# Reordering the hand-written queues at the entry of the first MLP product: token splits, weight splits and one split moved to GpSimd

## The chip, the cores and the metric

The kernel runs on one core of a Trainium2 chip. The metric is the device time of one execution, in microseconds (us). Before the change it was 1467.71 us, the median of three runs (1466.81 to 1469.4).

## The reference

One encoder layer over two sequences (1024 and 512 tokens, model width 1024) with shared weights, and a final RMSNorm. The part around the change is the end of the mixer and the start of the MLP:

```
x = x + gate1 * (mix @ w_out)
h = rms_norm(x, g_mlp) * (1 + scale2) + shift2
ff = square(relu(h @ w_ff1)) @ w_ff2          # w_ff1: 1024 x 4096
x = x + gate2 * ff
```

Everything is float32.

## The kernel before, in words

**Arithmetic.** Float32 products are made from three fp32r products: each operand v is split into v_hi (a copy in fp32r) and v_lo = v - v_hi, and each tile costs the matmuls w_lo*v_hi, w_hi*v_lo, w_hi*v_hi (`three_more`, L968 to L970). Both MLP products use a Strassen-Winograd scheme on 2x2 blocks with seven products, P1, P5, P6, P2, P7, P3, P4 in the order in which TensorE does them. The operands of the seven products are blocks of h or differences of such blocks.

**Chunks.** The 1536 tokens are three chunks of 512, done in the order 0, 2, 1. In the output projection TensorE makes eight groups of matmuls for a chunk (d = 0 to 7). For each group VectorE adds the result to x (L1949), ScalarE squares it (L1113, `square`), VectorE adds the squares up (L1611, `add_square`). The sum of squares of a chunk is summed over partitions by TensorE (`norm_sum`), becomes 1/rms by a ScalarE root and a VectorE reciprocal (L1617), and is spread over the partitions by TensorE (`norm_spread`). Then VectorE (`norm_apply`, L1910) and ScalarE (`modulate`, L1399) make h of the chunk, eight tiles of 128x512.

**Token operands, in two parts.** Part 0 is made from chunks 0 and 2 (operands of 128x2048), and is complete while TensorE still works on chunk 1. Part 1 is made from chunk 1 (128x1024). For each part: four differences on VectorE (`token_sum`, L1920 to L1929), seven hi copies on ScalarE (`token_hi`, L1409), seven lo subtractions on VectorE (`token_lo`, L1937). The hi copies share one counter, so `HI_ORDER` must repeat the order in which ScalarE makes them.

**Weights.** For each job q, SyncE loads four blocks of w_ff1; GpSimd makes four differences (`w1_add`, L2260 to L2274), ScalarE the hi copies (`split_w1_hi`, L1425), GpSimd the lo subtractions (`w1_split_lo`, L2284), all 128x512.

**Jobs.** Job 0 uses part 0 alone (512 columns); jobs 1 to 4 and most later ones use both parts (768 columns). TensorE makes P1 to P4 of a job; ScalarE copies the results of P1, P6, P7, P4 out of PSUM (`ff1_out`, L1434, counter `ff1_copy`); VectorE combines all of it in eleven steps, U2, C11, B11, C22, B22, C12, B12, T1, T3, T2, T4 (`hid_out`, L1985 to L2015, counter `hid_step`). P1, P6, P7 and P4 of a job take the same PSUM banks one after the other. These waits tie the engines together at the border between job 0 and job 1:

```
elif i == P2: after(pe, ff1_copy, 4 * q)
...
else: pe.wait_ge(ff1_copy, 4 * q + {P6: 1, P7: 2, P4: 3}[i])     # in ff1_product
...
after(act, hid_step, NHID * (q - 1) + step)                      # in ff1_out
ff1_out(q, P1, S_B11, T1)
```

So P6 of job 1 waits for the copy of P1 of job 1, and that copy, which writes over the slot `S_B11`, waits for step T1 of job 0. The copy of P6 waits for T2 of job 0, and TensorE's P1, P5 and P3 of job 1 wait for C11, C22 and C12 of job 0. All products of job 1 wait for the last `norm_apply` of chunk 1.

The order of the work on each engine is written out by hand. VectorE, ScalarE and GpSimd each take their instructions strictly in that order. For the change the relevant pieces are: the loop over the groups of chunk 1 (`for d in range(KD)` with i == 2 on VectorE; `square(n, k)` with n == NN + 2 on ScalarE), and the straight code behind it. `square(n, k)` with k > 2 waits until `add_square` has taken the buffer of k - 2, and `add_square(n, k)` waits for `square(n, k)`. The difference for P6 on GpSimd (L2268) waits in job 0 for group 4 of chunk 1 (`out_mm` at 2 * KD + 5).

Of the kernel before, what the change touches and what calls it, by code (L numbers as in the profile page):

```python
# [44 lines left out]
KD = D // P  # L45
# [24 lines left out]
P1, P5, P6, P2, P7, P3, P4 = range(7)  # L70
U2, C11, B11, C22, B22, C12, B12, T1, T3, T2, T4 = range(1, 12)

HI_ORDER = ((P1, P2, P3, P5, P6, P7, P4), (P1, P5, P6, P2, P3, P7, P4))
S_B11, S_T2, S_T3, S_T4, S_B21, S_T1, S_B22 = range(7)
NHID = 11
NSTEP = 7 * NPAIR // GF
# [37 lines left out]
def build_encoder(nc, vec_d, xT_d, w_mod_d, w_mod1_d, w_in_d, w_gate_d, w_four_d, w_out_d, w_ff1_d, w_ff2_d,  # L114
# [608 lines left out]
    def _(pe):  # L723
# [282 lines left out]
        for q in range(NJ):  # L1006
            for i in range(7):
                ff1_product(q, i)
                if q == 0 and i == P5:
                    norm_sum(2 * NN - 1)  # L1010
                elif q == 0 and i == P6:
                    norm_spread(2 * NN - 1)

        def fin_sum(h):
# [78 lines left out]
    def _(act):  # L1093
# [346 lines left out]
        for n in range(NN, 2 * NN):  # L1440
            if n > NN:
                root(n - 1)
            square(n, 0)
            if n > NN:
                modulate(n - 1)
            for k in range(1, KD):
                if n == NN + 1 and k == 3:
                    token_hi(P1, 0)
                    token_hi(P2, 0)
                elif n == NN + 2 and k == 2:  # L1450
                    token_hi(P3, 0)
                    split_w1_hi(0, P1)
                    token_hi(P5, 0)
                elif n == NN + 2 and k == 3:
                    token_hi(P6, 0)
                elif n == NN + 2 and k == 4:
                    token_hi(P7, 0)
                    split_w1_hi(0, P5)
                elif n == NN + 2 and k == 5:
                    split_w1_hi(0, P6)  # L1460
                    split_w1_hi(0, P2)
                elif n == NN + 2 and k == 6:
                    token_hi(P4, 0)
                square(n, k)

        def split_w2_hi(n):

# [55 lines left out]
        split_w1_hi(0, P3)  # L1523
        ff1_out(0, P6, S_T3, T2)
        split_w1_hi(0, P4)
        modulate(2 * NN - 1, range(4))
        split_w1_hi(1, P1)
        modulate(2 * NN - 1, range(4, KD))
        ff1_out(0, P7, S_B22, T2)
        token_hi(P1, 1)  # L1530
        split_w1_hi(1, P5)
        token_hi(P5, 1)
        split_w1_hi(1, P6)
        token_hi(P6, 1)
        split_w1_hi(1, P2)
        token_hi(P2, 1)
        ff1_out(0, P4, S_B21, T4)
        token_hi(P3, 1)
        for q in range(1, NJ):
            ff1_out(q, P1, S_B11, T1)  # L1540
            if q == 1:
                token_hi(P7, 1)
                token_hi(P4, 1)
            split_w1_hi(q, P7)
            split_w1_hi(q, P3)
            ff1_out(q, P6, S_T3, T2)
            split_w1_hi(q, P4)
            if q + 1 < NJ:
                split_w1_hi(q + 1, P1)
            else:  # L1550
                split_w2_hi(0)
                split_hin_hi(0)
            ff1_out(q, P7, S_B22, T2)
            if q + 1 < NJ:
                split_w1_hi(q + 1, P5)
                split_w1_hi(q + 1, P6)
            ff1_out(q, P4, S_B21, T4)
            if q + 1 < NJ:
                split_w1_hi(q + 1, P2)
# [30 lines left out]
    def _(dve):  # L1590
# [348 lines left out]
        for i in range(NCH):  # L1939
# [3 lines left out]
            for d in range(KD):  # L1943
# [12 lines left out]
                    add_square(NN + i, d - 1)  # L1956
                if i == 2 and d == 1:
                    token_sum(1, 0)
                    token_sum(2, 0)
                elif i == 2 and d == 2:  # L1960
                    token_lo(P1, 0)
                elif i == 2 and d == 3:
                    token_sum(3, 0)
                elif i == 2 and d == 4:
                    token_lo(P5, 0)
                elif i == 2 and d == 5:
                    token_sum(4, 0)
                elif i == 2 and d == 6:
                    token_lo(P6, 0)
            add_square(NN + i, KD - 1)  # L1970

        def hid_out(q, step):
# [128 lines left out]
            dve.wait_ge(norm_bc, 2 * NN + 2)  # L2101
            final(tiles, HTOK + CH, T, bank[7][:, 0:QC])

        token_lo(P2, 0)
        token_lo(P7, 0)
        rstd(2 * NN - 1)
        token_lo(P3, 0)
        norm_apply(2 * NN - 1, range(4))
        token_lo(P4, 0)
        norm_apply(2 * NN - 1, range(4, KD))  # L2110
        hid_out(0, U2)
        hid_out(0, C11)
        token_sum(1, 1)
        token_sum(2, 1)
# [2 lines left out]
        hid_out(0, C22)  # L2117
        token_lo(P5, 1)
        token_sum(3, 1)
        token_sum(4, 1)  # L2120
        for step in (B22, C12, B12, T1):
            hid_out(0, step)
        token_lo(P6, 1)
        token_lo(P2, 1)
        hid_out(0, T3)
        hid_out(0, T2)
        token_lo(P7, 1)
        token_lo(P3, 1)
        token_lo(P4, 1)
        hid_out(0, T4)  # L2130
        for q in range(1, NJ):
            for step in (U2, C11, B11):
                hid_out(q, step)
# [57 lines left out]
    def _(pool):  # L2191
# [51 lines left out]
        for i in range(16):  # L2243
# [2 lines left out]
                               wo_hi[WO_ORDER[i]][:].rearrange("p k m -> p (k m)"), ALU.subtract  # L2246
                               ).then_inc(wo_lo_done, 1)

        def w1_add(q, i):

            o = 7 * q + i
# [44 lines left out]
        for q in range(NJ):  # L2296
            w1_split_lo(q, P1)
            w1_add(q, P5)
            w1_add(q, P6)
            w1_split_lo(q, P5)  # L2300
            w1_split_lo(q, P6)
            w1_split_lo(q, P2)
            w1_add(q, P7)
            w1_add(q, P3)
            w1_split_lo(q, P7)
            w1_split_lo(q, P3)
            w1_split_lo(q, P4)
# [69 lines left out]
```

## Time and profile before

| | |
|---|---|
| median of three runs | 1467.71 us |
| range | 1466.81 to 1469.4 us |
| the profiled execution's own time | 1466.81 us |
| its span, from the first to the last instruction | 1465.0 us |
| mean granted TensorE clock | 0.990 |
| TensorE busy with matmuls | 1410.0 us (96%) |
| VectorE / ScalarE / GpSimd busy | 816.4 / 591.7 / 506.8 us |

TensorE is called PE in the rows, its weight loads PEld, VectorE DVE, ScalarE ACT, GpSimd POOL, and SyncE's queue SPq. A row of the timeline is: start, duration, engine, line, operation, output and inputs, and in brackets the idle time of the engine before it and what ended it. Wait tables infer the releaser from semaphore events; where an instruction waits for several things, they name the one that came last by the profile. Durations of two instructions in a row on one engine overlap by about 0.1 us, so the start-to-start distance is what a queue costs.

### The profile page before, as it was taken

To read this page: it belongs to the slowest core of one execution; us is meant where nothing else is said; L and a number is where in the kernel's file an instruction comes from. 1 tells how busy PE (TensorE), PEld (TensorE's weight loads), DVE (VectorE), ACT (ScalarE), POOL (GpSimd) and SP (SyncE) were. 2 spreads that over 40 slices of the span, in tenths; PEclk is the share of its full clock that TensorE was granted. 3 is DMA by queue.
4 is the path that set the end of the run, shared out by engine and by line. 5 is a ranking of instruction groups with operands and counts; after the bars stand their busy time and mean duration, and the time that the engine had idled before them with its cause. 6 is when DMAs were issued, how large, how long until landed. Compare 5 with 4: busy or idle time off the path is not lost.

```text
span 1465.0 us, 18563 instructions
## 1 busy us (share of the span) xinstructions
PE 1410.0 (96%) x7576; PEld 1190.6 (81%) x7576; DVE 816.4 (56%) x765; ACT 591.7 (40%) x704; POOL 506.8 (35%) x292
## 2 busy tenths in 40 slices
PE   3899999999999989999999999999999999999996
PEld 1576777788888878888888888888888888888885
DVE  5755687685536896353445344542655443344575
ACT  6448887846344443233222222242232222423231
POOL 6211111017200555565554555442223222232221
PEclk9899999999999999999999999999999999999998
DMA  9243431012512223433333333379998433445532
GB/s 370 87 159 133 156 121 36 15 58 84 203 58 87 87 88 138 153 133 130 119 115 147 142 119 117 147 244 390 393 377 312 159 144 144 161 180 207 209 134 86
DMA packets 75411, 232.35 MB, mean 159 GB/s; under 512 B 5696, under 2 KB 9920, under 8 KB 66368
## 3 DMA queue, kind: packets, MB, share of 16 engines
q1 hardware_dynamic: 75328, 231.17, 42.6%
q8 instruction: 61, 1.00, 0.3%
q14 instruction: 22, 0.18, 0.0%
HBM read 166.14 MB, written 65.01 MB: 158 GB/s over the span
## 4 chain that ended last, share of the span: by engine, by line
PE 52%; DVE 5%; issue 3%; SPq 2%; ACT 1%; DMA 1%; POOL 0%; DVEq 0%; ACTq 0%; POOLq 0%
PE bank L968 17%; PE bank L969 17%; PE bank L970 17%; DMA w_raw<-in_w_ff 1%; SPq L687 1%; DVE hin_lo L2036 1%; ACT hin_hi L1490 1%; DVE x L2086 1%; SPq L627 1%; DVE x L2052 0%; DVE hid L2000 0%; DVE w_raw L2031 0%; DVE w_raw L2029 0%; DVE w_raw L2027 0%; POOL w_lo L2284 0%
## 5 line engine op out<-in xcount | busy, mean ns | idle before, releaser
L968 PE MATMUL bank<-hin_hi,w_lo 128*128 128x512 f32 (+1 forms) x896 | 302.4, 337 | 1.8 <-DVE hin_lo L2036 1.8
L969 PE MATMUL bank<-hin_lo,w_hi 128*128 128x512 f32 (+1 forms) x896 | 301.7, 337 | 0.0
L970 PE MATMUL bank<-hin_hi,w_hi 128*128 128x512 f32 (+1 forms) x896 | 301.1, 336 | 0.0
L2036 DVE TENSOR_TENSOR hin_lo<-hin,hin_hi 128x3072 fp32r<-128x3072 f32 x28 | 140.9, 5031 | 208.1 <-ACT hin_hi L1490 208.1
L2292 POOL TENSOR_TENSOR w_lo<-w_raw,w_hi 128x2048 fp32r<-128x2048 f32 x28 | 129.5, 4625 | 330.5 <-ACT w_hi L1478 329.0
L968 PEld LDWEIGHTS bank<-hin_hi,w_lo 128*128 128x128 f32 x896 | 170.1, 190 | 21.0 <-issue 2.8
L969 PEld LDWEIGHTS bank<-hin_lo,w_hi 128*128 128x128 f32 x896 | 170.1, 190 | 17.8 <-issue 0.2
L970 PEld LDWEIGHTS bank<-hin_hi,w_hi 128*128 128x128 f32 x896 | 169.9, 190 | 17.9
L1478 ACT ACTIVATE w_hi<-w_raw 128x2048 fp32r<-128x2048 f32 x28 | 53.6, 1916 | 288.8 <-PE bank L970 181.6
L2284 POOL TENSOR_TENSOR w_lo<-w_raw,w_hi 128x512 fp32r<-128x512 f32 x51 | 73.9, 1449 | 206.6 <-ACT w_hi L1425 206.6
L1434 ACT ACTIVATE hid<-bank 128x768 f32<-128x768 f32 (+2 forms) x68 | 52.5, 772 | 170.4 <-PE bank L970 163.3
L968 PE MATMUL bank<-t_hi,w_lo 128*128 128x512 f32 (+1 forms) x320 | 112.2, 351 | 6.3 <-DVE t_lo L1937 3.7
L969 PE MATMUL bank<-t_lo,w_hi 128*128 128x512 f32 (+1 forms) x320 | 112.1, 350 | 0.0
L970 PE MATMUL bank<-t_hi,w_hi 128*128 128x512 f32 (+1 forms) x320 | 111.6, 349 | 0.0
L2284 POOL TENSOR_TENSOR w_lo<-w_s,w_hi 128x512 fp32r<-128x512 f32 x68 | 103.2, 1530 | 10.0 <-ACT w_hi L1425 6.5
L1985 DVE TENSOR_TENSOR hid<-bank,hid 128x768 f32<-128x768 f32 (+2 forms) x17 | 15.5, 910 | 147.1 <-ACT hid L1434 147.1
L2207 POOL TENSOR_TENSOR win_lo<-win_raw,win_hi 128x1024 fp32r<-128x1024 f32 x12 | 30.8, 2565 | 192.0 <-ACT win_hi L1136 192.0
L968 PE MATMUL bank<-hi_f,w_lo 128*128 128x512 f32 (+1 forms) x256 | 86.6, 338 | 1.9 <-POOL w_lo L2284 1.9
L968 PE MATMUL bank<-hi_r,w_lo 128*128 128x512 f32 (+1 forms) x256 | 87.2, 341 | 0.0
L1425 ACT ACTIVATE w_hi<-w_s 128x512 fp32r<-128x512 f32 x68 | 42.9, 632 | 109.3 <-POOL w_s L2274 47.6
L969 PE MATMUL bank<-lo_r,w_hi 128*128 128x512 f32 (+1 forms) x256 | 86.9, 339 | 0.0
L969 PE MATMUL bank<-lo_f,w_hi 128*128 128x512 f32 (+1 forms) x256 | 86.5, 338 | 0.0
(271 smaller groups left out, 3204.2 us busy)
## 6 DMA issues: line engine op xcount, KB each, us to landing
hin<-hid_all SPq DMA_DIRECT2D x28, 1536.0 KB, 6.6
hid_all<-hid SPq DMA_DIRECT2D x105, 384.0 KB, 2.5
w_raw<-in_w_ff SPq DMA_DIRECT2D x36, 1024.0 KB, 9.0
w_raw<-in_w_ff SPq DMA_DIRECT2D x68, 256.0 KB, 2.8
mod_raw<-in_w_mod SPq DMA_DIRECT2D x16, 1024.0 KB, 5.1
x<-in_xT SPq DMA_DIRECT2D x5, 2048.0 KB, 14.0
w_sums<-w_raw SPq DMA_DIRECT2D x8, 1024.0 KB, 15.4
w_raw<-w_sums SPq DMA_DIRECT2D x8, 1024.0 KB, 10.4
```

The lines of the kernel that those rows point to most:

```text
L627: sp.dma_start(w2_raw[m % RAWS][:], src).then_inc(ld_w2[m % RAWS], 16)
L968: pe.matmul(out, w_lo, v_hi, start=first, stop=False, skip_group_check=True)
L969: pe.matmul(out, w_hi, v_lo, start=False, stop=False, skip_group_check=True)
L970: return pe.matmul(out, w_hi, v_hi, start=False, stop=last, skip_group_check=True)
L1425: act.activation(w1_hi[o % 4][:], src[:], ACT.Copy).then_inc(w1_hi_done, 1)
L1434: act.activation(hid[j][:, c0:c1], ps[:, buf + c0:buf + c1], ACT.Relu if i == P4 else ACT.Copy).then_inc(ff1_copy, 1)
L1478: act.activation(w2_hi[n % 2][:], w2_raw[m % RAWS][:], ACT.Copy).then_inc(w2_hi_done, 1)
L1985: m = dve.tensor_tensor(slot[S_T3][:, cols], out_of(1), slot[S_T3][:, cols], ALU.add)
L2036: dve.tensor_tensor(hin_lo[n % 3][:].rearrange("p t n -> p (t n)"), hin[n % 3][:].rearrange("p t n -> p (t n)"), hin_hi[n % 3][:].rearrang ...
L2207: pool.tensor_tensor(win_lo[win_of(j)][:].rearrange("p k m -> p (k m)"), raw[:], win_hi[win_of(j)][:].rearrange("p k m -> p (k m)"), ALU.s ...
L2284: pool.tensor_tensor(w1_lo[o % 4][:], src[:], w1_hi[o % 4][:], ALU.subtract).then_inc(w1_lo_done, 1)
L2292: pool.tensor_tensor(w2_lo[n % 2][:].rearrange("p t n -> p (t n)"), w2_raw[m % RAWS][:].rearrange("p t n -> p (t n)"), w2_hi[n % 2][:].rea ...
```

## The change

Work is moved between places in the queues of ScalarE, VectorE and TensorE, and one subtraction moves to another engine. No work is added or removed.

- ScalarE, part 0: the hi copies come in the order P1, P2, P5, P3, P6, P7, P4. In front of the square of tile 3 of chunk 1 there are now the weight hi copies of P1, P5, P6 and P2 of job 0 and the token hi copies of P3 and P6; P7's is in front of the square of tile 4, and P4's behind the last square.
- VectorE, part 0: the lo subtraction of P2 moves into the loop, the differences move to later groups, the lo subtraction of P7 leaves VectorE; GpSimd does it, between its weight subtraction for P2 and its difference for P7 of job 0.
- TensorE: the spreading of the last norm comes behind P2 of job 0 instead of P6.
- VectorE, part 1: `norm_apply` is done in one piece, behind U2 of job 0; the five lo subtractions of P6, P2, P7, P3 and P4 come in front of T1 of job 0, and T1, T3, T2, T4 close the sequence. C12 and B12 stand between the subtractions of P2 and P7.
- ScalarE, part 1: the copy of P7 of job 0 comes after four tiles of `modulate` instead of eight; weight hi copies come in front of the token hi copies; the token hi copies of P7 and P4 come in front of the copy of P1 of job 1.

```diff
-HI_ORDER = ((P1, P2, P3, P5, P6, P7, P4), (P1, P5, P6, P2, P3, P7, P4))
+HI_ORDER = ((P1, P2, P5, P3, P6, P7, P4), (P1, P5, P6, P2, P7, P3, P4))
...
                 if q == 0 and i == P5:
                     norm_sum(2 * NN - 1)
-                elif q == 0 and i == P6:
+                elif q == 0 and i == P2:
                     norm_spread(2 * NN - 1)
...
                 elif n == NN + 2 and k == 2:
-                    token_hi(P3, 0)
-                    split_w1_hi(0, P1)
                     token_hi(P5, 0)
                 elif n == NN + 2 and k == 3:
+                    split_w1_hi(0, P1)
+                    token_hi(P3, 0)
+                    split_w1_hi(0, P5)
+                    split_w1_hi(0, P6)
+                    split_w1_hi(0, P2)
                     token_hi(P6, 0)
                 elif n == NN + 2 and k == 4:
                     token_hi(P7, 0)
-                    split_w1_hi(0, P5)
-                elif n == NN + 2 and k == 5:
-                    split_w1_hi(0, P6)
-                    split_w1_hi(0, P2)
-                elif n == NN + 2 and k == 6:
-                    token_hi(P4, 0)
                 square(n, k)
+        token_hi(P4, 0)
...
         split_w1_hi(0, P4)
-        modulate(2 * NN - 1, range(4))
+        modulate(2 * NN - 1, range(2))
         split_w1_hi(1, P1)
+        modulate(2 * NN - 1, range(2, 4))
+        ff1_out(0, P7, S_B22, T2)
         modulate(2 * NN - 1, range(4, KD))
-        ff1_out(0, P7, S_B22, T2)
+        split_w1_hi(1, P5)
         token_hi(P1, 1)
-        split_w1_hi(1, P5)
+        split_w1_hi(1, P6)
         token_hi(P5, 1)
-        split_w1_hi(1, P6)
+        ff1_out(0, P4, S_B21, T4)
+        split_w1_hi(1, P2)
         token_hi(P6, 1)
-        split_w1_hi(1, P2)
         token_hi(P2, 1)
-        ff1_out(0, P4, S_B21, T4)
+        token_hi(P7, 1)
         token_hi(P3, 1)
+        token_hi(P4, 1)
         for q in range(1, NJ):
             ff1_out(q, P1, S_B11, T1)
-            if q == 1:
-                token_hi(P7, 1)
-                token_hi(P4, 1)
...
                 if i == 2 and d == 1:
                     token_sum(1, 0)
+                elif i == 2 and d == 2:
                     token_sum(2, 0)
-                elif i == 2 and d == 2:
                     token_lo(P1, 0)
                 elif i == 2 and d == 3:
                     token_sum(3, 0)
-                elif i == 2 and d == 4:
                     token_lo(P5, 0)
                 elif i == 2 and d == 5:
                     token_sum(4, 0)
+                    token_lo(P6, 0)
                 elif i == 2 and d == 6:
-                    token_lo(P6, 0)
+                    token_lo(P2, 0)
...
-        token_lo(P2, 0)
-        token_lo(P7, 0)
+        token_lo(P3, 0)
         rstd(2 * NN - 1)
-        token_lo(P3, 0)
-        norm_apply(2 * NN - 1, range(4))
         token_lo(P4, 0)
-        norm_apply(2 * NN - 1, range(4, KD))
         hid_out(0, U2)
+        norm_apply(2 * NN - 1)
         hid_out(0, C11)
...
         token_lo(P5, 1)
         token_sum(3, 1)
+        hid_out(0, B22)
         token_sum(4, 1)
-        for step in (B22, C12, B12, T1):
-            hid_out(0, step)
         token_lo(P6, 1)
         token_lo(P2, 1)
-        hid_out(0, T3)
-        hid_out(0, T2)
+        for step in (C12, B12):
+            hid_out(0, step)
         token_lo(P7, 1)
         token_lo(P3, 1)
         token_lo(P4, 1)
-        hid_out(0, T4)
+        for step in (T1, T3, T2, T4):
+            hid_out(0, step)
...
+        def token_lo(i, part):                                   # on GpSimd
+
+            v, v_hi, v_lo = token_operand(i, part)
+            pool.wait_ge(op_hi, hi_count(i, part))
+            pool.wait_ge(op_sum, 4 * part + {P1: 1, P7: 3, P3: 3, P4: 4}[i])
+            pool.tensor_tensor(v_lo, v, v_hi, ALU.subtract).then_inc(op_lo[i], 1)
...
             w1_split_lo(q, P2)
+            if q == 0:
+                token_lo(P7, 0)
             w1_add(q, P7)
```

## Rows read from the trace of the kernel before

**Rows 1.** The page: busy time, share of the span, instructions.

```profile
PE 1410.0 (96%) x7576; PEld 1190.6 (81%) x7576; DVE 816.4 (56%) x765; ACT 591.7 (40%) x704; POOL 506.8 (35%) x292
```

**Rows 2.** Waits of TensorE, whole span: total us, times, longest us.

```profile
PE bank L968 <- DVE t_lo L1937: 3.7, 1, 3.7
PE bank L968 <- issue: 2.6, 1, 2.6
PE bank L968 <- POOL w_lo L2284: 1.9, 1, 1.9
```

**Rows 3.** Windows: engines' busy time, then granted clock, DMA share, GB/s.

```profile
515.00:520.00 5.00, 3.37 (x10) 2.73 (x11) 4.90 (x6) 5.00 (x8) 3.16 (x3) 0.77 0.00 0
650.00:655.00 5.00, 5.00 (x30) 5.00 (x31) 3.26 (x7) 1.09 (x3) 3.70 (x3) 0.66 0.43 135
```

**Rows 4.** Timeline of TensorE around job 0 and job 1.

```profile
500.75 0.95 PE L739 MATMUL bank<-ones,n_acc 128*128 128x1 f32 x8
...
516.63 0.47 PE L968 MATMUL bank<-t_hi,w_lo 128*128 128x512 f32 x1 [2.64 <-issue]
516.94 0.40 PE L969 MATMUL bank<-t_lo,w_hi 128*128 128x512 f32 x1
517.18 0.39 PE L970 MATMUL bank<-t_hi,w_hi 128*128 128x512 f32 x1
...
518.83 0.63 PE L969 MATMUL bank<-t_lo,w_hi 128*128 128x512 f32 x1
519.26 0.63 PE L970 MATMUL bank<-t_hi,w_hi 128*128 128x512 f32 x1
...
533.25 0.47 PE L968 MATMUL bank<-t_hi,w_lo 128*128 128x512 f32 x1 [3.68 <-DVE t_lo L1937]
```

**Rows 5.** Timeline of VectorE from the last norm to step T1 and behind it.

```profile
506.44 0.74 DVE L1910 SCALAR_TENSOR_TENSOR n_t<-x,amp,bank 128x512 f32<-128x512 f32 x1
...
515.10 0.68 DVE L1985 TENSOR_TENSOR hid<-bank,hid 128x512 f32<-128x512 f32 x1
...
530.35 1.64 DVE L2004 TENSOR_TENSOR hid<-hid,hid 128x512 f32<-128x512 f32 x1
531.91 1.21 DVE L1937 TENSOR_TENSOR t_lo<-t_s,t_hi 128x1024 fp32r<-128x1024 f32 x1
533.05 1.21 DVE L1937 TENSOR_TENSOR lo_r<-h_r,hi_r 128x1024 fp32r<-128x1024 f32 x1
```

**Rows 6.** Timeline of ScalarE.

```profile
468.30 0.63 ACT L1425 ACTIVATE w_hi<-w_raw 128x512 fp32r<-128x512 f32 x1 [1.72 <-PE bank L728]
468.84 1.90 ACT L1409 ACTIVATE t_hi<-t_s 128x2048 fp32r<-128x2048 f32 x1
470.64 0.61 ACT L1113 ACTIVATE tmp<-x 128x512 f32<-128x512 f32 x1
...
532.07 0.81 ACT L1434 ACTIVATE hid<-bank 128x768 f32<-128x768 f32 x1 [7.19 <-DVE hid L2004]
```

**Rows 7.** Timeline of GpSimd in the loop over chunk 1.

```profile
479.32 1.30 POOL L2268 TENSOR_TENSOR w_s<-w_s,w_raw 128x512 f32<-128x512 f32 x1 [7.30 <-PE bank L728]
```

**Rows 8.** Timeline of VectorE in the loop over chunk 1.

```profile
474.10 0.74 DVE L1949 SCALAR_TENSOR_TENSOR x<-bank,mod,x 128x512 f32<-128x512 f32 x1
474.76 0.68 DVE L1611 TENSOR_TENSOR n_acc<-n_acc,tmp 128x512 f32<-128x512 f32 x1
475.36 2.28 DVE L1926 TENSOR_TENSOR h_f<-h_r,h_f 128x2048 f32<-128x2048 f32 x1
...
497.02 0.69 DVE L1611 TENSOR_TENSOR n_acc<-n_acc,tmp 128x512 f32<-128x512 f32 x1 [0.17 <-ACT tmp L1113]
```

**Rows 9.** Timeline of GpSimd and VectorE in the second product, near 1000 us.

```profile
987.94 3.36 DVE L2036 TENSOR_TENSOR hin_lo<-hin,hin_hi 128x3072 fp32r<-128x3072 f32 x1 [6.21 <-ACT hin_hi L1490]
...
996.65 4.62 POOL L2292 TENSOR_TENSOR w_lo<-w_raw,w_hi 128x2048 fp32r<-128x2048 f32 x1 [10.44 <-ACT w_hi L1478]
...
999.26 5.24 DVE L2036 TENSOR_TENSOR hin_lo<-hin,hin_hi 128x3072 fp32r<-128x3072 f32 x1 [7.96 <-ACT hin_hi L1490]
```

## The prediction

> **What bounds the kernel now.** I read the page first: TensorE is busy 96% of the span [rows 1], so an order of instructions can only win or lose where TensorE idles. The wait table of TensorE gives two waits in the stretch of the change, 2.6 and 3.7 us, and one of 1.9 us in a later job [rows 2]. The timeline places them: 2.64 us before P4 of job 0, which starts at 516.63, and 3.68 us before P6 of job 1, which starts at 533.25 [rows 4]. Behind the first one the granted clock falls: 0.77 of full speed from 515 to 520, and matmuls start 0.43 us apart instead of 0.24 [rows 3, 4], the lower level, 1.2 GHz, instead of 2.4. About 8 matmuls are hit, some 1.6 us. The 1.9 us wait is followed by such a stretch too (0.66 from 650 to 655) [rows 3].
>
> Then the question is which wait ends last. The table names a split, t_lo at L1937, for 533.25. The code and ScalarE's timeline say otherwise: P6 of job 1 needs `ff1_copy` 5, the copy of P1 of job 1. That copy stood on ScalarE for 7.19 us and began at 532.07, released by L2004, step T1 of job 0 [rows 6]; T1 ran from 530.35 to 531.99 [rows 5], the copy ended at 532.88. The split of P6 for part 1 ended at 533.12, but the first matmuls of P6 are on part 0 and don't need it. So the path that sets the end runs along VectorE up to T1, through ScalarE's copy, into TensorE at 533.25. Everything that TensorE gains or loses before it ends in that wait: the 2.64 us and the slow stretch of P4 are already hidden by it. Behind it TensorE has no wait until the one of 1.9 us, which moves along with TensorE, since that job's weights wait on TensorE's own progress.
>
> **The change part by part.** The measure is the time at which T1 of job 0 is done.
>
> *T1 behind the splits of part 1.* VectorE's stream from U2 at 515.10 to the end of T1 at 531.99 took 16.9 us [rows 5]. U2 moves in front of the norm (-0.6). Five 1024-wide subtractions (P6, P2, P7, P3, P4) come in front of T1. One costs 1.14 us of queue (531.91 to 533.05), so 5 x 1.14 = 5.7; where GpSimd is in the way one can take double, which is the upper bound, 11.4. I take 5.7, because GpSimd's next work (the weight subtractions of P7 of job 1) hangs behind the copy that hangs behind T1, so it is idle then. Net: +5.1.
>
> *P7's split on GpSimd.* It takes 4.62 us there by the row of the same shape [rows 9], against 2.28 for a 2048-wide operation on VectorE [rows 8]. VectorE is spared 2.2 us. But while GpSimd works, a VectorE operation with two inputs in SBUF stands still: the 3072-wide subtraction takes 3.36 us alone and 5.24 us when it began at 999.26 beside GpSimd's 4.62 from 996.65, and it ended at 1004.50, 3.23 after GpSimd's end at 1001.27. It waited for all of the rest of it [rows 9]. The Trainium skill (SBUF — State Buffer, "Who interferes with whom") has this as a rule: the port pair that VectorE and GpSimd share is an exclusive lock for a whole instruction, and a VectorE instruction with two SBUF inputs needs it. The trace agrees (1.9 us of waiting). By that rule 4.62 us can be lost to the add behind it; if the two only shared bandwidth, about half of that.
>
> *The new order on ScalarE.* The weight hi copy of P6 now stands in front of the square of tile 3. It needs the difference that GpSimd may begin at 479.32 at the earliest, when group 4 is done, and that takes 1.30 [rows 7]. Worked through, with 0.66 for an add to x, 0.60 for an add of squares, 2.2 for a 2048-wide operation on VectorE [rows 8], 0.54 and 1.80 for the short and the long hi copies on ScalarE [rows 6]:
> - Group 2 is done at 468.30 [rows 6]. VectorE does x, add, difference 2, split P1, x, add, difference 3: 0.66 + 0.6 + 2.2 + 2.2 + 0.66 + 0.6 + 2.2 = 9.1, and about 1.7 for two GpSimd operations in the way: 479.1. Then the split of P5 to 481.4. GpSimd's difference waits for it and is done at 482.6.
> - ScalarE: two weight copies, the hi of P6 (1.8), square 3 to about 486.1, the hi of P7 to 487.9, square 4 to 488.5. VectorE has stood idle for the add of square 3 from 482 to 486.1.
> - GpSimd takes P7's split at 488.0 and holds the port to 492.6. The add of square 4 (ready at 488.6) waits for it: 493.2. Difference 4, split P6, x of group 6, add (behind a GpSimd operation, 1.8), split P2, x of group 7: 502.8. The last two adds: 504.8. Before, the last add ended at 497.71 [rows 8].
> - TensorE would have begun the norm's sum at 500.75 [rows 4]; it begins at 504.8, a new wait of 3.8 us, hidden like the 2.64. P6 (behind ScalarE's late copy of P1, 506.0) and P2 at 2.7 each and the spreading end at 512.1. `norm_apply` begins then instead of at 506.44 [rows 5]; its eight tiles, with the copies between them on ScalarE, take about 6.5, to 518.6. Before, its end with P4's split in the middle was 515.10. Net: +3.5. If nothing early is late, the sum is at 500.75, the spreading at 507.7, the tiles end at 514.2, and this term is -0.9; if the clock falls in the wait before the sum, it is +5.1.
>
> *TensorE's slow stretch.* P6 of job 1 will start about 533.25 + 5.1 + 3.5 = 541.9. P5 ends near 532, so the idle time is nearly 10 us, more than either wait of before. I expect the lower clock level behind it, now on the path: +1.6 (8 matmuls at 0.19 more each, the measured stretch [rows 4]). The bounds are 0, as behind the 3.68 us wait, and 1.7.
>
> *Costed at nothing.* The earlier copy of P7 takes the 2.64 us wait away, but P4 of job 0 is hidden by the wait before P6. The weight hi copies of job 1 moved forward, and the loads of job 2, which SyncE sends behind T4 of job 0: T4 ends at about the same time as before, and TensorE needs them over 8 us later. The copy of P6 of job 1 waits for T2 and a store, and both are due before the late P6 ends. The cover of all of this is the wait before P6; without it they would cost up to 2 us each.
>
> The sum against the profiled execution's own time: 1466.81 + 5.1 + 3.5 + 1.6 = **1477.0 us**. The median of the runs is 0.9 above that execution, which the range takes in.
>
> **Rivals.**
> - *The early part stays hidden.* If GpSimd's difference gets in front of P5's split (it is late by only 0.2 us in my working) or P7's split finds the port free, the early term lies between -0.9 and +1.5: 1466.8 + 5.1 + 0.3 + 1.6 gives about 1473.8, down to 1471.0. For it: the race is close, and adds on VectorE are short. Against: the square of tile 3 still can't come before 484 or so.
> - *No change.* From U2 to T1 VectorE's work alone is six 1.14 us units, eight short steps of 0.6 and 0.5 between dependent ones, 12.1 us, against the 16.9 that it took: 4.8 us went to GpSimd's turns at the port. If the new order met none of them, norm_apply would end at 514.2 and T1, with C11, eleven 1.14 us units of differences and splits and six short steps, at 514.2 + 0.6 + 12.5 + 3.6 + 0.8 = 531.7, against 531.99. That is 1466.5. It needs every port wait gone, with GpSimd's work unchanged.
> - *Faster.* The wait table is right and the code's reading wrong: the split L1937 releases P6 of job 1, not T1. Then the split, with P7's 2.2 us off VectorE, is done at about 530.9 instead of 533.1, and 2.2 us are gained: 1464.6. It decides if P6 of job 1 starts before T1 has ended. Against it stands a counter that TensorE must wait for.
>
> **How the numbers follow.** My working: 0.65. Early part hidden: 0.20. No change: 0.09. Faster: 0.04, and 0.02 for a still later chain. About 0.2% (2.9 us) is what a measurement of this kernel can tell from no change. Faster 0.04, same 0.10, slower 0.86. The likeliest case spans 1475 (no slow stretch) to 1480.4 (two slow stretches and the median's 0.9 on top). The range goes down to 1471.0 for the second case and leaves about 0.15 out.
>
> **What would show it.** Right: one long wait of TensorE, 8 to 11 us, before P6 of job 1 at 540 to 543, released by the copy at L1434; T1 (L2004) directly behind L1937 rows, ending near 540.6; a wait of 3 to 4 us before the sum at L739 near 504; a GpSimd row of 128x2048 with 4.6 us near 488 and an add (L1611) of over 4 us beside it; no wait before P4 of job 0. Wrong: P6 of job 1 before 536, the sum at 501, or the slow stretch missing behind the long wait.

## The result, and the profile after

The changed kernel took 1481.59 us (median of six runs, 1479.63 to 1485.63) against 1468.57 us for the kernel before on the same chip: ratio 1.0094, 95% interval 1.0076 to 1.0112. It is slower, as forecast, but by more than forecast: 1477.0 had been named, with 1480.4 as the upper end. The profiled execution is not one of these six: it took 1484.28 us, its span 1482.5, 17.5 longer than the 1465.0 of before.

Waits of TensorE in the changed kernel, whole span (engine, line, releaser: us in total, times, longest us). They answer to [rows 2]:

```profile
PE bank L968 <- ACT hid L1434: 10.2, 1, 10.2
...
PE bank L739 <- DVE n_acc L1609: 3.2, 1, 3.2
...
PE bank L968 <- DVE lo_f L1935: 2.2, 1, 2.2
PE bank L968 <- POOL w_lo L2286: 1.9, 1, 1.9
```

Timeline of TensorE in the changed kernel, the counterpart of [rows 4]:

```profile
509.32 1.87 PE L739 MATMUL bank<-ones,n_acc 128*128 128x1 f32 x8 [3.25 <-DVE n_acc L1609]
511.05 0.77 PE L968 MATMUL bank<-t_hi,w_lo 128*128 128x512 f32 x1
...
514.61 0.63 PE L970 MATMUL bank<-t_hi,w_hi 128*128 128x512 f32 x1
515.04 0.53 PE L968 MATMUL bank<-t_hi,w_lo 128*128 128x512 f32 x1
...
549.76 0.77 PE L968 MATMUL bank<-t_hi,w_lo 128*128 128x512 f32 x1 [10.16 <-ACT hid L1434]
550.33 0.63 PE L969 MATMUL bank<-t_lo,w_hi 128*128 128x512 f32 x1
```

The norm's sum (L739) has a wait of 3.25 us in front of it, and takes 1.87 us instead of the 0.95 of [rows 4]. P6 of job 1 starts at 549.76 behind 10.16 us of waiting, and the table now names ScalarE's copy at L1434, the releaser that the code had given for the kernel before too.

VectorE, the counterpart of [rows 5, 8]:

```profile
461.25 0.75 DVE L1947 SCALAR_TENSOR_TENSOR x<-bank,mod,x 128x512 f32<-128x512 f32 x1 [2.32 <-PE bank L728]
...
490.77 0.83 DVE L1609 TENSOR_TENSOR n_acc<-n_acc,tmp 128x512 f32<-128x512 f32 x1 [4.16 <-ACT tmp L1113]
491.52 0.74 DVE L1947 SCALAR_TENSOR_TENSOR x<-bank,mod,x 128x512 f32<-128x512 f32 x1
493.10 4.61 DVE L1609 TENSOR_TENSOR n_acc<-n_acc,tmp 128x512 f32<-128x512 f32 x1 [0.84 <-ACT tmp L1113]
...
519.63 0.75 DVE L1908 SCALAR_TENSOR_TENSOR n_t<-x,amp,bank 128x512 f32<-128x512 f32 x1 [2.26 <-PE bank L746]
...
526.00 0.68 DVE L1987 TENSOR_TENSOR hid<-bank,hid 128x512 f32<-128x512 f32 x1
...
546.69 1.22 DVE L1935 TENSOR_TENSOR t4b_lo<-t4b_s,t4b_hi 128x1024 fp32r<-128x1024 f32 x1
547.82 0.68 DVE L2002 TENSOR_TENSOR hid<-hid,hid 128x512 f32<-128x512 f32 x1
```

ScalarE and GpSimd of the same kernel:

```profile
487.19 0.63 ACT L1425 ACTIVATE w_hi<-w_s 128x512 fp32r<-128x512 f32 x1 [5.47 <-POOL w_s L2270]
...
490.05 0.62 ACT L1113 ACTIVATE tmp<-x 128x512 f32<-128x512 f32 x1
...
548.59 0.81 ACT L1434 ACTIVATE hid<-bank 128x768 f32<-128x768 f32 x1 [7.68 <-issue]
```

```profile
484.01 3.08 POOL L2270 TENSOR_TENSOR w_s<-w_s,w_raw 128x512 f32<-128x512 f32 x1 [3.02 <-PE bank L728]
...
492.55 4.60 POOL L2249 TENSOR_TENSOR lo_f<-h_f,hi_f 128x2048 fp32r<-128x2048 f32 x1 [1.50 <-ACT hi_f L1409]
```

Read together, these show the foreseen chain. GpSimd's difference begins where it did before (484.01, less the 4.70 us of which the next paragraph tells, is 479.31; before it was 479.32 [rows 7]), but it takes 3.08 us instead of 1.30, beside VectorE's split of P5, which ran until 485.95, so it ends late. ScalarE's weight copy waits 5.47 us for it. VectorE's add of square 3 waits 4.16 us, and the add of square 4 stands 4.61 us beside GpSimd's 4.60 us split. At the end, T1 (L2002) stands directly behind the splits, and the copy at L1434 behind T1.

**What the trace adds.** The first add to x of chunk 1 starts at 461.25, but the kernel before had it earlier:

```profile
456.55 0.75 DVE L1949 SCALAR_TENSOR_TENSOR x<-bank,mod,x 128x512 f32<-128x512 f32 x1 [2.32 <-PE bank L728]
```

Nothing ahead of this point was changed. The windows say where the 4.70 us went (columns as in [rows 3]); first the kernel before, then the changed one:

```profile
320.00:325.00 5.00, 5.00 (x40) 4.85 (x41) 5.00 (x9) 5.00 (x9) 0.00 (x0) 1.00 0.01 3
325.00:330.00 5.00, 5.00 (x25) 4.05 (x23) 5.00 (x8) 3.21 (x7) 2.75 (x3) 1.00 0.00 0
```

```profile
320.00:325.00 5.00, 5.00 (x28) 5.00 (x28) 5.00 (x9) 5.00 (x9) 0.00 (x0) 0.57 0.01 3
325.00:330.00 5.00, 5.00 (x18) 4.32 (x18) 5.00 (x8) 3.23 (x7) 1.67 (x2) 0.50 0.00 0
...
510.00:515.00 5.00, 5.00 (x15) 4.17 (x16) 4.70 (x3) 3.05 (x8) 2.93 (x2) 0.50 0.93 304
```

From 320 to 330 the granted clock is at its lower level in the changed kernel's profile, in untouched code. So I measure by a **distance**: from the first add to x of chunk 1 on VectorE to the start of P6 of job 1 on TensorE. It was 533.25 - 456.55 = 76.70 us and is 549.76 - 461.25 = 88.51 us. The 17.5 us are 4.70 ahead of it, 11.81 in it, and 1.0 behind it. The distance ends where P6 starts, so it doesn't hold what the clock costs behind that start. Where that matters I give a second measure, from the same first add to the end of the span: 1008.45 us before, 1021.25 changed, 12.8 more.

### The profile page after: what moved, and what is told of

Same layout as the page of the kernel before. It is cut to its first block, busy times and chain, and to the rows that moved or that the text cites. A ratio compares the mean times of both kernels' runs of the same rounds, so it can differ in the third digit from the quotient of the medians.

```text
span 1482.5 us, 18562 instructions
## 1 busy us (share of the span) xinstructions
PE 1417.1 (96%) x7576; PEld 1197.4 (81%) x7576; DVE 809.4 (55%) x764; ACT 591.4 (40%) x704; POOL 503.4 (34%) x293
## 4 chain that ended last, share of the span: by engine, by line
PE 58%; DVE 2%; issue 2%; ACT 1%; POOL 0%; DVEq 0%; ACTq 0%; POOLq 0%
PE bank L968 19%; PE bank L969 19%; PE bank L970 19%; DVE x L2084 1%; ACT hin_hi L1488 1%; DVE w_raw L2029 0%; DVE hin_lo L2034 0%; POOL w_lo L2286 0%; DVE fin_acc L2068 0%; DVE x L2050 0%; DVE fin_acc L2060 0%; ACT fin_sq L1502 0%; PE bank L1025 0%; ACT fin_b L1510 0%; POOL w_s L2272 0%
## 5 line engine op out<-in xcount | busy, mean ns | idle before, releaser
L1434 ACT ACTIVATE hid<-bank 128x768 f32<-128x768 f32 (+2 forms) x68 | 52.5, 772 | 181.2 <-PE bank L970 173.6
L968 PE MATMUL bank<-t_hi,w_lo 128*128 128x512 f32 (+1 forms) x320 | 113.4, 354 | 11.2 <-ACT hid L1434 10.2
L2286 POOL TENSOR_TENSOR w_lo<-w_s,w_hi 128x512 fp32r<-128x512 f32 x68 | 97.4, 1444 | 18.6 <-ACT w_hi L1425 15.1
L1998 DVE SCALAR_TENSOR_TENSOR hid<-hid 128x768 f32<-128x768 f32 (+2 forms) x51 | 86.5, 1696 | 1.7
## 6 DMA issues: line engine op xcount, KB each, us to landing
w_raw<-w_sums SPq DMA_DIRECT2D x8, 1024.0 KB, 10.2
```

Source lines behind the costliest of these rows:

```text
L968: pe.matmul(out, w_lo, v_hi, start=first, stop=False, skip_group_check=True)
L1434: act.activation(hid[j][:, c0:c1], ps[:, buf + c0:buf + c1], ACT.Relu if i == P4 else ACT.Copy).then_inc(ff1_copy, 1)
L1998: m = dve.scalar_tensor_tensor(t, t, 0.0, t, ALU.max, ALU.mult)
L2286: pool.tensor_tensor(w1_lo[o % 4][:], src[:], w1_hi[o % 4][:], ALU.subtract).then_inc(w1_lo_done, 1)
```

## The experiments

Line numbers differ by a few between kernels. The kernel before had a median of 1469.58 us (13 runs) beside the first four kernels, 1469.89 (23 runs) beside the two with fillers and the two at the end, and 1469.71 (23 runs) beside the other three.

**The late part alone.** The kernel before, with VectorE's order behind `token_sum(3, 1)` and the token hi copies of part 1 in the changed kernel's order:

```diff
+        hid_out(0, B22)
         token_sum(4, 1)
-        for step in (B22, C12, B12, T1):
-            hid_out(0, step)
         token_lo(P6, 1)
         token_lo(P2, 1)
-        hid_out(0, T3)
-        hid_out(0, T2)
+        for step in (C12, B12):
+            hid_out(0, step)
         token_lo(P7, 1)
         token_lo(P3, 1)
         token_lo(P4, 1)
-        hid_out(0, T4)
+        for step in (T1, T3, T2, T4):
+            hid_out(0, step)
```

> The kernel before with the late part alone: on VectorE the five lo subtractions of part 1 stand in front of T1 of job 0, with ScalarE's token hi copies of P7 and P4 in front of the copy of P1 of job 1. Mark for all runs: D, from the start of VectorE's add to x of group 0 of chunk 1 to the start of P6 of job 1 on TensorE; 76.7 us in the kernel before, 88.5 in the changed one. Theory (T1 is what P6 of job 1 waits for, and it is moved behind 5 x 1.14 us): D 81.8 to 82.5, the wait before P6 of job 1 grows from 3.7 to about 9 us, the norm's sum on TensorE without a new wait, and with a slow stretch behind the wait the time is 7 us above before. Rival (the early part carries the loss, the splits in front of T1 are free because VectorE has slack): D 76.7 and no change of time.

Measured: 1475.39 us, ratio 1.005 (1.0033 to 1.0067); distance 82.38, +5.7. T1 behind the splits costs what five splits were priced at, 5.7, with nothing early in play. TensorE:

```profile
539.19 0.77 PE L968 MATMUL bank<-t_hi,w_lo 128*128 128x512 f32 x1 [10.76 <-ACT hid L1434]
```

**T1 put back in the changed kernel** (the diff above, reversed, on the VectorE side).

> The changed kernel with VectorE's late sequence put back (B22, C12, B12, T1 in front of the five lo subtractions), all else as changed. Theory: T1 ends about 6 us earlier, D 82 to 83, wait before P6 of job 1 about 4 us, the wait of 3 us before the norm's sum still there with its slow stretch; time about 6 us above before and 7 below the changed kernel. Rival (early part carries the loss): D stays near 88.

Measured: 1477.22 us, ratio 1.0054 (1.0035 to 1.0073); distance 82.20, 6.3 less than in the changed kernel. To the end of the span it is 4.5 less (1016.76): the slow stretch behind P6's start is longer here. The early part stays: the sum waits 3.25 us, as in the changed kernel.

**P7's split back on VectorE in the changed kernel.**

```diff
+        token_lo(P7, 0)
         token_lo(P3, 0)
         rstd(2 * NN - 1)
...
-            if q == 0:
-                token_lo(P7, 0)
             w1_add(q, P7)
```

> The changed kernel with the lo subtraction of P7 of part 0 back on VectorE, behind the last add of squares. Theory (GpSimd's 4.6 us hold the port against the add of square 4, and that delays the sum): the add of square 4 takes 0.7 instead of 4.6, the norm's sum starts with a wait under 1 us and no slow stretch behind it; VectorE pays 2.2 us for the subtraction; D 83 to 86, time 7 to 10 us above before. Rival (only ScalarE's new order delays the sum): the wait before the sum stays near 3 us, D 88 or more.

Measured: 1476.05 us, ratio 1.0055 (1.0034 to 1.0076); distance 83.09, 5.4 less, and, with a longer slow stretch behind P6's start here too, 3.8 less to the end of the span (1017.48). VectorE:

```profile
485.85 0.82 DVE L1609 TENSOR_TENSOR n_acc<-n_acc,tmp 128x512 f32<-128x512 f32 x1 [4.17 <-ACT tmp L1113]
486.60 0.74 DVE L1947 SCALAR_TENSOR_TENSOR x<-bank,mod,x 128x512 f32<-128x512 f32 x1
488.18 0.69 DVE L1609 TENSOR_TENSOR n_acc<-n_acc,tmp 128x512 f32<-128x512 f32 x1 [0.84 <-ACT tmp L1113]
```

The wait for square 3 is there (4.17), the next add is short (0.69 instead of 4.61), and TensorE's sum has no wait and takes 0.95 us. So the idle time that ScalarE's order causes doesn't by itself delay the sum.

**The weight copies back behind squares 4 and 5 on ScalarE in the changed kernel.**

```diff
                     token_hi(P3, 0)
-                    split_w1_hi(0, P5)
-                    split_w1_hi(0, P6)
-                    split_w1_hi(0, P2)
                     token_hi(P6, 0)
                 elif n == NN + 2 and k == 4:
                     token_hi(P7, 0)
+                    split_w1_hi(0, P5)
+                elif n == NN + 2 and k == 5:
+                    split_w1_hi(0, P6)
+                    split_w1_hi(0, P2)
```

> The changed kernel with the weight hi copies of P5, P6 and P2 of job 0 back at their places on ScalarE (in front of the squares of tiles 4 and 5). Theory (two causes in a row): VectorE's idle time of 4.2 us for the add of square 3 is gone, but GpSimd's subtraction of P7 still stands in front of an add or a difference; the sum is 1 to 2 us earlier than in the changed kernel, D 86 to 87.5. Rival (ScalarE's order is the whole early cause): the wait before the sum is gone and D is 83 or less. Rival (GpSimd is the whole cause): D unchanged, 88.5.

Measured: a median of 1481.86 us, ratio 1.0089 (1.0069 to 1.0108), hardly below the changed kernel's. The profiled execution took 1474.93 us, with a distance of 83.97, 4.5 less, more than expected. GpSimd's hold now falls on a split of VectorE, the sum waits 1.96 us instead of 3.25 and takes 1.05, not 1.87:

```profile
489.45 6.51 DVE L1936 TENSOR_TENSOR t_lo<-t_s,t_hi 128x2048 fp32r<-128x2048 f32 x1
```

```profile
502.93 1.05 PE L739 MATMUL bank<-ones,n_acc 128*128 128x1 f32 x8 [1.96 <-DVE n_acc L1610]
```

The other runs don't bear this out. The profiled one is the fastest of six; the others lie from 1479.70 to 1485.48. Whether the stretch behind the 1.96 us wait runs slow in the others is open, so what the weight copies' place is worth is not shown.

**Matmuls in the waits.** Two kernels keep TensorE busy in its waits with matmuls whose results nothing uses: `fill` sends `count` of them into a PSUM bank that is free at that time. The first kernel puts 14 before the norm's sum, the second also 38 before P6 of job 1.

```diff
+        def fill(count, i, q):
...
+            for n in range(count):
+                pe.matmul(bank[NBK][:], w1_hi[o % 4][:, 0:P], v_hi[:, n % FT], start=True, stop=True)
...
+                if q == 1 and i == P6:                 # the second kernel alone
+                    fill(38, P6, 1)
...
                 if q == 0 and i == P5:
+                    fill(14, P6, 0)
                     norm_sum(2 * NN - 1)
```

> The changed kernel with 14 extra matmuls of 512 columns on TensorE behind P5 of job 0, in the 3.25 us for which it waits for the last norm's sum (into the norm's own bank, which the sum writes anew). They add no work to VectorE, ScalarE or GpSimd. Theory (the wait is followed by the lower clock, and P6 and the sum at that clock delay the spreading, norm_apply and so T1): clock 1.00 from 510 to 515, sum in 0.95 us instead of 1.87, norm_apply 2 to 2.8 us earlier, D 85.7 to 86.5, time 2 to 3 us below the changed kernel. Rival (the lower clock there is hidden as it was at P4 in the kernel before): D 88.5.

> As the run before, and 38 more matmuls of 512 columns in the wait of 10 us before P6 of job 1. Theory: D as in the run before (85.7 to 86.5), no lower clock behind the wait, and the rest of the program from P6 of job 1 to the end takes 1.3 to 1.7 us less: time 3.5 to 4.5 us below the changed kernel. Rival (the clock behind that wait costs nothing, since a later wait takes it up): the rest takes as long as in the changed kernel.

Measured: 1478.63 us, ratio 1.0065 (1.0049 to 1.008), and 1477.81 us, 1.0056 (1.0039 to 1.0073). With the first filler the sum starts at the same distance (48.1) but takes 1.05 us, the first `norm_apply` tile comes at 56.06 instead of 58.38 behind the first add to x, and the whole distance is 86.20: 2.3 us less. More than half of this is lost again behind it. All 12 matmuls of 512 columns that open P6 of job 1, and four of 256 behind them, run at the lower clock here, where in the changed kernel it is the first six or seven; whether the filler has to do with that is open. To the end of the span 1020.25 us are left of 1021.25, a gain of 1.0, and the intervals of the two ratios overlap. So the trace shows what the sum's slow stretch costs on the path; the runs don't show a faster kernel. Windows of the first filler kernel, where the changed kernel has 0.50 behind its sum:

```profile
505.00:510.00 5.00, 4.71 (x24) 3.93 (x24) 5.00 (x4) 4.20 (x11) 2.95 (x2) 1.00 0.90 295
510.00:515.00 5.00, 5.00 (x22) 3.80 (x21) 2.98 (x5) 1.80 (x3) 2.31 (x2) 1.00 0.53 182
```

The second filler takes the slow stretch behind the long wait away as well. From the start of P6 of job 1 to the 1.93 us wait of the next job it is 116.60 us in the kernel before, 118.06 in the changed one, and 116.63 here. The distance stays at 86.25. To the end of the span it is 1017.62, 3.6 less than in the changed kernel, the lower end of what was expected.

**Both causes undone at once.** The changed kernel with the edits of the second and third experiments; ScalarE's and TensorE's new orders stay.

> The changed kernel with both causes undone: T1 of job 0 stands where it stood before the change, and VectorE makes the lo subtraction of P7 of part 0. ScalarE's and TensorE's new orders stay. Theory (two causes that add up, no third): from the first add to x of chunk 1 to the start of P6 of job 1, 88.5 us less 5.4 (P7 alone undone) less 6.3 (T1 alone undone) is 76.8 us, against 76.7 before the change; the sum starts on time at 44.2; the median is within 0.2% of the kernel before, ratio 0.999 to 1.002. Rival (the new ScalarE order costs something by itself, since putting it back gave 4.5 us): 78 to 80 us, the first norm_apply tile 2 to 3 us later than before, ratio 1.002 to 1.004.

Measured: 1470.08 us, ratio 1.0011 (0.9998 to 1.0024); distance 76.77. In the distance the two undo steps add up, and nothing is left: 88.51 - 6.3 - 5.4 = 76.8. To the end of the span it is 1009.63, 1.2 above the kernel before: behind its 3.88 us wait P6 meets the lower clock, where before it met none.

**P7's split on GpSimd in the kernel before**, all else as it was.

> The kernel before with one edit: the lo subtraction of P7 of part 0 goes from VectorE to GpSimd, between its weight subtraction for P2 and its difference for P7. Theory (the move costs nothing by itself; what costs is that in the changed kernel the split meets the adds of squares late and with the sum waiting on them): one add of squares takes over 4 us here too, but the sum starts on time at 44.2 us after the first add to x, norm_apply is not later than before (49.9) and may be 1 us earlier, and P6 of job 1 starts 75.7 to 76.7 us after it; ratio 0.998 to 1.001. Rival (the port hold always costs its 4.6 us less the 2.3 saved): P6 of job 1 at 78.5 to 79.5 us, the sum 2 to 4 us late, ratio 1.0015 to 1.003.

Measured: 1468.82 us, ratio 0.999 (0.9976 to 1.0003); distance 75.59, a little below what was expected, with the sum on time at 44.2. To the end of the span it is 1009.67, again 1.2 above the kernel before, for the same reason (P6 of job 1, below). An add is held here too, and it does no harm:

```profile
490.51 3.76 DVE L1611 TENSOR_TENSOR n_acc<-n_acc,tmp 128x512 f32<-128x512 f32 x1
```

**The changed kernel once more.**

> The changed kernel once more, unchanged. Theory (of its 17.5 us, 4.7 belong to a half-clock stretch at 321 to 331 us in code that the change does not touch, and it is drawn anew in each execution): in this profile the first add to x of chunk 1 starts at 456.3 to 456.8 us, or at 459.5 to 461.5 if the stretch is drawn again; in both cases P6 of job 1 starts 88 to 89 us behind it; the runs fall in two groups some 3 to 5 us apart, the fast one at 1479 to 1481. Rival (the stretch belongs to the changed kernel): the first add at 461.2 again and no run under 1482 beside it; or P6 of job 1 at another distance.

Measured: 1480.13 us, ratio 1.0081 (1.0061 to 1.01); the profiled execution took 1485.23. The slow stretch began earlier this time, the first add to x came at 462.14, P6 of job 1 at 550.53, distance 88.39. Windows of this execution:

```profile
315.00:320.00 5.00, 4.88 (x34) 4.88 (x35) 4.76 (x9) 4.08 (x7) 0.00 (x0) 0.78 0.00 0
320.00:325.00 5.00, 5.00 (x26) 5.00 (x25) 4.04 (x8) 4.31 (x7) 0.00 (x0) 0.50 0.02 3
```

My bounds for the start (459.5 to 461.5) were missed by 0.6. The rival, that no run would be under 1482, fell: the changed kernel has fourteen executions on record, twelve in the two medians and two more of 1484.28 (the first profiled one) and 1484.59. Seven lie from 1479.63 to 1480.74, one at 1482.43, six from 1484.28 to 1485.63. Both profiles happen to be of the slower kind, and without the stretch they would have taken 1484.28 - 4.70 = 1479.6 and 1485.23 - 5.6 = 1479.6 us.

**A version that is better than both.** The kernel before with P7's split on GpSimd, and with two differences of part 1 behind T1 instead of in front:

```diff
-        token_sum(3, 1)
-        token_sum(4, 1)
         for step in (B22, C12, B12, T1):
             hid_out(0, step)
+        token_sum(3, 1)
+        token_sum(4, 1)
```

> The kernel before with two edits: on VectorE, differences 3 and 4 of part 1 go behind T1 of job 0 (B22, C12, B12, T1, then the differences), and the lo subtraction of P7 of part 0 goes to GpSimd. Theory (T1 is the end of the path): T1 comes earlier by 2 x 1.14 us and some of GpSimd's turns, D 73.5 to 74.5, time 2 to 3 us below before. GpSimd's 4.6 us fall between 487 and 492, where one difference or add of squares waits, but the sum is not late. Rival (what is moved comes back as a wait for the split of P6, as the wait table names it): D 76 or more.

Measured: 1465.68 us, ratio 0.9975 (0.9963 to 0.9988), twelve runs. The distance is 72.40, less than expected, and 1005.06 to the end of the span (3.4 less than before), with a wait of 0.76 us in P6, where the split of its part 1 operand is now last:

```profile
528.84 0.47 PE L968 MATMUL bank<-t_hi,w_lo 128*128 128x512 f32 x1 [1.89 <-ACT hid L1434]
532.58 0.36 PE L968 MATMUL bank<-t_hi,w_lo 128*128 128x256 f32 x1 [0.76 <-DVE t_lo L1937]
```

A further kernel rewrote the order of VectorE from the last norm on, and ScalarE's with it, so that T1 and the splits come each just before they are needed. Its core on VectorE against the kernel just shown:

```diff
-        token_lo(P5, 1)
-        for step in (B22, C12, B12, T1):
-            hid_out(0, step)
         token_sum(3, 1)
+        hid_out(0, B22)
+        hid_out(0, C12)
+        hid_out(0, B12)
+        token_lo(P5, 1)
+        hid_out(0, T1)
         token_sum(4, 1)
...
+        hid_out(0, T4)
         token_lo(P3, 1)
         token_lo(P4, 1)
-        hid_out(0, T4)
```

> The kernel before with GpSimd's subtraction of P7 and a new order of VectorE and ScalarE from the copy of P1 of job 0 on: norm_apply earlier, the copy of P7 behind four tiles of it, U2, B11, B22, C12, B12 and T1 as early as their inputs allow, each lo subtraction of part 1 shortly before TensorE needs it. The loop over chunk 1 is left as it was. Theory: no wait of TensorE over 2.2 us in this stretch, so the clock stays up; several short waits (before P1, P5, P6 and P7 of job 1) with 4 us in sum instead of 6.3; D 72 to 73.5, time 4 us below before. Rival (the path goes back to waits for the splits): D 75 or more.

Measured: 1465.00 us, ratio 0.9972 (0.9961 to 0.9984), no better than the simpler one within the intervals. The distance is 74.06, above the 72 to 73.5 expected. P6 starts without a wait, but P5 of job 1 now waits in front of its part 1, longer than the 2.2 us that no wait was to exceed, and its twelve matmuls behind that run at the lower clock (0.21 apart, where they are 0.12 apart at the full one):

```profile
530.88 0.55 PE L968 MATMUL bank<-t_hi,w_lo 128*128 128x256 f32 x1 [2.56 <-DVE t_lo L1941]
```

A split now bounds this place beside T1; that VectorE's queue as a whole is what is left is my reading, not tried.

## Why the prediction was right in direction and too low in size

*The path.* Right. T1, the copy at L1434, P6 of job 1, in that order, and the wait table of the kernel before had named another releaser [rows 2]. With T1 put back and nothing else the distance fell by 6.3 us. The rival "faster" needed P6 of job 1 to start before T1 had ended; it started 1.3 us behind that end. In all thirteen profiles P6 of job 1 starts 0.36 or 0.37 us behind the end of the copy at L1434, also where the wait table names a split (532.88 to 533.25 in the kernel before): the copy is the gate.

*T1 behind the splits, +5.1.* Right, 0.5 too low: from the end of `norm_apply` to the end of T1 it was 531.99 - 515.10 = 16.9 us and is 548.50 - 526.00 = 22.5, +5.6. Alone it cost 5.7 (first experiment). Four of the five splits took 1.22 us as the row chosen said, and one, beside GpSimd, 2.27; the upper bound of 11.4 was not touched.

*The early part, +3.5.* The step that failed. Its beginning held: taking off the 4.70 us, the adds were to end at 504.8 and the sum began at 509.32 - 4.70 = 504.62, with a wait of 3.25 where 3.8 was worked out. But the tiles of `norm_apply` began at 519.63 - 4.70 = 514.93 instead of 512.1, and ended at 521.30 instead of 518.6: +6.2 against the 515.10 of before, beyond even the bound of +5.1. I had taken the clock to stay up in the wait before the sum and had put its fall into the bound alone, at 1.6 us. It fell, and it hit the sum (1.87 instead of 0.95) besides nine matmuls of P6 at 0.43 apart. The filler kernel prices this at 2.3 us of the path; 0.5 more are spread over the rest. The evidence stood in [rows 2 to 4]: a 2.64 us wait had dropped the clock, a 3.68 us wait had not, and I took the wrong one of the two as the model where the late sum is on the path. Undoing P7's move took 5.4 off, not 6.2, because 0.7 of the 6.2 is there without it: U2, moved in front of the norm, no longer stands behind it, and the late part has that back.

*The slow stretch behind the wait before P6 of job 1, +1.6.* Right: 118.06 - 116.60 = 1.46 us, and with the filler it is gone. From there to the end the changed kernel takes 814.68 us and the kernel before 815.15; the thirteen profiles lie from 814.35 to 815.33, so these 0.5 us are no more than profiles differ by. That leaves the 1.0 of the account above. The term can't be read closer than this: behind waits of 3.6 to 10.8 us the stretch from P6's start to the 1.93 us wait took 116.60 to 119.45 us.

*Costed at nothing.* Right for the earlier copy of P7 (the wait before P4 of job 0 is gone and bought nothing), the weight copies of job 1 and the loads: with the two causes undone all of these stay in and the distance is 76.77 against 76.70 (the 1.2 us more that follow come from the lower clock behind P6's start).

*The sum.* 6.2 + 5.6 + 1.0 = 12.8 us where 10.2 had been forecast, so 1466.81 + 12.8 = 1479.6. That is what both profiled executions give without the stretch at 320 us, and close to where seven of fourteen executions lie. The median of the first six came out 2.0 higher. That this is the stretch, drawn slow in some executions, is argued from the two groups of runs some 5 us apart; only the profiled ones show it. The runs of the kernel before spread likewise; their median beside these was 1468.57, 1.8 above the execution that my sum started from. So of the 4.6 us between 1477.0 and 1481.59, 1.8 come from the base and 2.8 from the change, which the runs put at 13.0 and the traces at 12.8. No term of mine covered the stretch: nothing in the one trace of before showed it, only the width of the runs could have hinted at it, and I added 0.9 for the median. So the range ended at the two slow stretches I had allowed for, 1.2 us under the median. Even that end was not what its terms give: 1477.0 + 1.6 + 0.9 is 1479.5, not 1480.4.

*The rivals.* "The early part stays hidden" named as one of its conditions that P7's split finds the port free. The third experiment is that case: with the split on VectorE the sum was on time. "No change" needed all port waits gone; they were not.

*What the early cost is made of.* Neither of its two causes costs anything in the distance alone. ScalarE's new order without GpSimd's split (and without the late T1) leaves the distance at 76.77; GpSimd's split in the old order leaves it at 75.59. Together they cost 5.4. My reading is that the order on ScalarE opens a hole in front of the adds of squares (4.17 us even where the sum is on time), and that GpSimd's 4.6 us take the slack that would have made up for it; how large that slack is was not measured. The Trainium skill (SBUF — State Buffer, "Who interferes with whom") says that a VectorE instruction with two SBUF inputs needs the port pair that GpSimd holds for its whole instruction; the 4.61 us add beside the 4.60 us split agrees, and so do the 6.51 us split and the 3.76 us add.

## What to carry to other kernels

Price a held port by what stands queued behind it, not by its length: the same 4.6 us cost nothing in one order and took part in 5.4 in another. Where a new wait of TensorE comes to lie on the path, count the lower clock behind it into the sum, and include in it the small matmuls that come first, as long as any wait of about its size in the same trace was followed by one. When two profiles are compared, measure between two events that enclose the change, and look first at whether the code ahead of it took the same time. Then look behind the second event too: the filler won 2.3 us up to P6 and had 1.0 of them left at the end.

## What the runs showed of the hardware

A stretch of small matmuls near 320 us, where no wait is over 0.69 us, ran at the full clock in seven of thirteen profiles and at the lower level for some 7 to 13 us in the other six, in kernels that are the same up to there; it cost 3.1 to 5.6 us, read from the start of the first add to x against the 456.55 of the kernel before. It is the largest single difference between executions that these traces show.

The length of a wait doesn't settle what follows. Behind 3.25 us (before the sum) the clock was down at once. Behind 2.64 us (before P4 of job 0, kernel before) it fell 1.3 us later. Behind 1.96 us it fell before P4 of job 0 with only P7's split on GpSimd, from 517.17 on, but not before the sum with the weight copies put back; behind 1.98 us before P4 of job 0, in the first of the two faster kernels, it didn't either. Nor does the place settle it. P6 of job 1 starts behind 3.68 us at the full clock in the kernel before [rows 4], and behind 3.63 us at the lower one with P7's split on GpSimd:

```profile
531.92 0.76 PE L968 MATMUL bank<-t_hi,w_lo 128*128 128x512 f32 x1 [3.63 <-DVE t_lo L1937]
532.48 0.63 PE L969 MATMUL bank<-t_lo,w_hi 128*128 128x512 f32 x1
```

Behind the same wait of 3.88 us, the first matmul of P6 took 0.77 us in the kernel with T1 put back, and 0.47 us with both causes undone, where the clock fell 1.2 us later:

```profile
543.44 0.77 PE L968 MATMUL bank<-t_hi,w_lo 128*128 128x512 f32 x1 [3.88 <-DVE t_lo L1935]
```

```profile
538.14 0.47 PE L968 MATMUL bank<-t_hi,w_lo 128*128 128x512 f32 x1 [3.88 <-DVE t_lo L1935]
```

In the first of these kernels TensorE had already waited 3.25 us before the sum; whether that matters wasn't tried by itself.

GpSimd is held by VectorE as well: its split of P7 took 4.60 us in the changed kernel, and 6.67 in the old order, where a VectorE difference of 3.37 us (instead of about 2.28) began 1.2 us ahead of it.
